# Attention values projected once per key block, and one MLP chunk computed by eight products instead of seven

## The reference, cut to what matters

```python
# attention, per layer; kv has 128 latent channels, 8 heads, w_uv[h] is 128 x 64
logits = einsum("bthc,btkc->bthk", q, kv_sel) * 128 ** -0.5 + bias
probs  = softmax(where(valid, logits, -inf))
o      = einsum("bthk,btkc->bthc", probs, kv_sel)   # 128 numbers per head
o      = einsum("bshc,hcd->bshd", o, w_uv)          # 64 numbers per head
x      = x + gate * rmsnorm(concat([y_conv, o * silu(g_attn)]) @ w_out)   # gate = part of silu(c) @ w_ada + b_ada
# MLP of the last layer, 1024 -> 4096 -> 1024
x      = x + square(relu(rmsnorm(x) @ w_up)) @ w_down
```

## Time and profile before

| | us |
|---|---|
| median of 3 runs (3002.47 to 3008.8) | 3005.6 |
| the profiled execution, device time | 3001.2 |
| its span in the trace | 2999.1 |
| PE busy with matmuls | 2766.2 (92%) |
| DVE busy | 2103.7 (70%) |
| ACT busy | 1417.0 (47%) |
| POOL busy | 1594.1 (53%) |

### The profile page before, as it was taken

One profiled execution on the slowest core, in us unless ns is written; L12 is line 12 of the kernel. 1 busy time (PEld: TensorE's weight loads), 2 busy tenths in 40 slices (PEclk: granted clock), 3 DMA queues, 4 the chain that ended last, 5 costly groups with the idle time before them and its releaser, 6 DMA issues.

```text
span 2999.1 us, 49452 instructions
## 1 busy us (share of the span) xinstructions
PE 2766.2 (92%) x19234; PEld 1706.8 (57%) x19442; DVE 2103.7 (70%) x3421; ACT 1417.0 (47%) x2541; POOL 1594.1 (53%) x1228
## 2 busy tenths in 40 slices
PE   6889989989879989989999999999999979999998
PEld 3459658754449668864566565665664434444443
DVE  5599987754599987644865665666654597777776
ACT  4366646533366746643344554454543343333333
POOL 4204669961504570012646956757662558888882
PEclk8999999999999999999999999999999989999999
DMA  7102433331202330022101211201123101111111
GB/s 274 46 1 86 141 102 120 101 131 50 95 1 81 123 118 23 23 82 78 43 29 43 71 43 32 82 29 57 57 74 124 57 29 57 57 57 56 57 57 63
DMA packets 50904, 213.49 MB, mean 71 GB/s; under 512 B 4680, under 2 KB 9968, under 8 KB 34032
## 3 DMA queue, kind: packets, MB, share of 16 engines
q1 hardware_dynamic: 42288, 195.63, 18.9%
q10 hardware_dynamic: 8384, 14.68, 1.5%
HBM read 190.36 MB, written 19.94 MB: 70 GB/s over the span
## 4 chain that ended last, share of the span: by engine, by line
PE 35%; DVE 8%; POOL 3%; issue 3%; ACT 1%; DMA 0%; DVEq 0%; ACTq 0%; POOLq 0%
PE big L303 8%; PE big L304 8%; PE big L302 7%; PE banks L1239 3%; PE banks L302 2%; PE banks L303 2%; PE banks L304 2%; POOL w_lo L638 2%; DVE arena L2899 2%; PE banks L1209 0%; PE banks L1218 0%; DVE arena L2880 0%; DVE arena L2805 0%; DVE arena L2726 0%; DVE arena L2884 0%
## 5 line engine op out<-in xcount | busy, mean ns | idle before, releaser
L725 POOL TENSOR_TENSOR w_lo<-stage,w_hi 128x512 bf16<-128x512 f32 x276 | 357.6, 1330 | 324.0 <-ACT w_hi L1475 323.7
L718 POOL CAST w_hi<-stage 128x512 bf16<-128x512 f32 x188 | 139.0, 782 | 592.2 <-PE big L304 465.0
L638 POOL TENSOR_TENSOR w_lo<-stage,w_hi 128x512 bf16<-128x512 f32 x174 | 249.6, 1445 | 260.9 <-ACT w_hi L1671 260.9
L302 PE MATMUL big<-w_hi,ht_hi 128*128 128x256 bf16 (+2 forms) x1272 | 352.5, 285 | 15.8 <-DVE ht_lo L2576 4.4
L303 PE MATMUL big<-w_lo,ht_hi 128*128 128x256 bf16 (+2 forms) x1274 | 353.5, 286 | 4.0 <-issue 3.7
L304 PE MATMUL big<-w_hi,ht_lo 128*128 128x256 bf16 (+2 forms) x1276 | 354.2, 286 | 0.3
L302 PE MATMUL big<-ht_hi,w_hi 128*128 128x512 bf16 x846 | 323.7, 383 | 26.2 <-POOL w_lo L638 8.5
L303 PE MATMUL big<-ht_lo,w_hi 128*128 128x512 bf16 x877 | 334.9, 382 | 12.5 <-DVE ht_lo L2154 10.1
L304 PE MATMUL big<-ht_hi,w_lo 128*128 128x512 bf16 x879 | 335.7, 382 | 1.0 <-issue 0.2
L303 PE MATMUL big<-arena,w_hi 128*128 128x512 bf16 (+1 forms) x783 | 249.2, 333 | 11.9 <-DVE arena L2323 8.0
L302 PE MATMUL big<-arena,w_hi 128*128 128x512 bf16 (+1 forms) x776 | 246.1, 332 | 14.9 <-DVE arena L2237 6.2
(11 more groups left out here) (416 smaller groups left out, 7795.0 us busy)
## 6 DMA issues: line engine op xcount, KB each, us to landing
stage<-in_w SPq DMA_DIRECT2D x130, 1024.0 KB, 4.9
arena<-in_w_ada SPq DMA_DIRECT2D x48, 512.0 KB, 3.9
arena<-in_x SPq DMA_DIRECT2D x16, 512.0 KB, 8.1
xs<-arena SPq DMA_DIRECT2D x16, 512.0 KB, 2.6
arena<-xs SPq DMA_DIRECT2D x16, 512.0 KB, 7.5
gt<-arena ACTq DMA_DIRECT2D x16, 256.0 KB, 2.8
arena<-gt ACTq DMA_DIRECT2D x16, 256.0 KB, 2.7
out_x<-arena SPq DMA_DIRECT2D x8, 512.0 KB, 2.6
```

The lines of the kernel that those rows point to most:

```text
L302: pe.matmul(out, ah, bh, start=start, stop=False, skip_group_check=onto)
L638: return pool.tensor_tensor(lo, x, hi, ALU.subtract)
L718: pool.tensor_copy(w_flat[0][:, w0 + c0:w0 + c1], stage[:, n % RAW_RING, c0:c1]).then_inc(s_w_hi_split, mark(s_w_hi_split, n, q))
L725: ins = pool.tensor_tensor(w_flat[1][:, w0 + c0:w0 + c1], stage[:, n % RAW_RING, c0:c1], w_flat[0][:, w0 + c0:w0 + c1], ALU.subtract)
```

## The change

1. Values. `values(s)` makes KV @ w_uv for key block s and all heads once (three matmuls of 512 columns), ahead of the loop for block 0 and after head 1 of block s-1 for the others; ACT and DVE split it into `VAL`. `weigh` now holds the probabilities still and streams 64 columns of `VAL`, all eight heads into one bank, one round later than before (i-4); `turn` is one round later too (i-2). The split of the weighed result, the 64-column product, its copy and the key transposes with their split are gone. `PB` gets a third buffer. DVE scales the whole block straight from PSUM. `turn_y` and the late sums move from the pool "big" to a bank of their own ("x").
2. Order. DVE does the low part of `PT` and of the queries ahead of the mask of the round; `turn_y` is at i-7.
3. Modulation. The group (0, 4) is computed at the start on PE by `ada_piece`, its four pieces loaded early; seven groups are left for POOL, which scales a piece by one tensor_tensor in place of two tensor_scalar, in rounds 20, 31, 39, 44, 51, 56, 63 in place of 20, 28, 36, 42, 48, 54, 58, 62. The gate row of layer 1 is multiplied at (1, 5), the last group.
4. MLP. Chunk 3 of `up` is computed by eight products; token sums 2 and 3 come after the first `down` pair.

```diff
-STRASSEN = range(3, 16)
+STRASSEN = range(4, 16)
-        pools = {..., "t": one[0:2], "o": one[2:4], "c": one[0:3], "f": one[3:4], "c2": two[2:4], "mlp": two}
+        pools = {..., "t": one[0:2], "o": one[2:4], "c": one[0:3], "pt": one[0:2], "ov": one[2:3], "x": one[3:4], "f": one[3:4], "c2": two[2:4], "mlp": two}
-        ADA_LATE = [(0, 4), (0, 5), (1, 4), (1, 5), (1, 0), (1, 1), (1, 2), (1, 3)]
-        ADA_STEP = dict(zip((20, 28, 36, 42, 48, 54, 58, 62), ADA_LATE))
+        ADA_LATE = [(0, 5), (1, 0), (1, 1), (1, 2), (1, 3), (1, 4), (1, 5)]
+        ADA_STEP = dict(zip((20, 31, 39, 44, 51, 56, 63), ADA_LATE))
...
 POOL, late_sums:
-                    for k in range(2):
-                        pool.tensor_scalar(x[:, k, :], x[:, k, :], s_(S_C + 2 * kp + k), None, ALU.mult)...
+                    pool.tensor_tensor(x, x, s_(S_C + 2 * kp, 2).unsqueeze(2).broadcast_to((P, 2, 512)), ALU.mult)...
 PE, transpose_x, behind the last transposes:
+                        if half and kp == 3:
+                            g = take(pe, "c", "gate4")
+                            for i in range(16, 20):
+                                ada_piece(i, g)
 PE, before the scores:
-                g = take(pe, "big", "kvtok", l)
-                for s in range(NT):
-                    ins = pe.transpose(g[:, s * P:(s + 1) * P], RAW[:, s * P:(s + 1) * P], ident)
 PE, attention:
+                def values(s):
+                    g = take(pe, "x", "v", l, s)
+                    mm3(pe, g, [x[:, s * P:(s + 1) * P] for x in KVT], [x[:, 0, 0:512] for x in uv], True, True)...
-                        ins = mm3(pe, g[:, 0:P], [x[:, s, :] for x in KVK], [x[:, s * P:(s + 1) * P] for x in PT[h % 2]], s == 0, s == tb)
+                        ins = mm3(pe, g, [x[:, s * P:(s + 1) * P] for x in PT[h % 2]], [x[:, s, h * 64:(h + 1) * 64] for x in VAL], s == 0, s == tb)
-                def values(tb, h, g):
-                    pe.wait_ge(s_ot_lo, when(s_ot_lo, l, tb, h))
-                    ins = mm3(pe, g[:, P:P + 64], OT[h % 2], [x[:, 0, h * 64:h * 64 + 64] for x in uv], True, True)
...
-                    if 3 <= i < n + 3:
-                        weigh(*steps[i - 3], g)
-                    if 5 <= i < n + 5:
-                        values(*steps[i - 5], g)
-                    if 1 <= i <= n:
-                        turn(*steps[i - 1])
+                    if 4 <= i < n + 4:
+                        weigh(*steps[i - 4])
+                    if 2 <= i < n + 2:
+                        turn(*steps[i - 2])
...
+                    if i < n and steps[i][1] == 1 and steps[i][0] < NT - 1:
+                        values(steps[i][0] + 1)
 ACT, MLP:
-                    evac(RT[n], ACT.Relu, "up", j, n, pool="mlp")
+                    evac(RT[n], ACT.Relu, "up", j, n, pool="mlp" if j < 3 else "big")
+                    sums_high("dn", 2, 0, 1, 2, 5, 4)
+                    token_sums(2, {2: lambda: sums_high("dn", 2, 3)})
+                    up_plain(3, (0,))
+                    token_sums(3, {1: lambda: sums_high("dn", 2, 6)})
+                    up_plain(3, (1,))
 DVE, MLP:
             token_sums(0)
             token_sums(1)
             square_parts(0)
-            token_sums(2)
             square_parts(1)
-            token_sums(3, lambda t: add_down(0, "p1", t - 3) if 3 <= t < 7 else None)
             for m in range(7):
                 down(m)
-                up_first(2 * m + 3)
+                if m:
+                    up_first(2 * m + 3)
+                else:
+                    square_low(2, "a22")
+                    token_sums(2)
+                    token_sums(3)
                 if m < 6:
                     up_second(2 * m + 4)
```

More of the change, by code:

```diff
@@ L603, in late_sums @@
             def late_sums():
-                for i in range(16, len(ADA_PIECES)):
+                for i in range(20, len(ADA_PIECES)):
                     l, n, kp = ADA_PIECES[i]
@@ L1089, in _ @@
                 queries(0)
-                for i in range(n + 8):
-                    if 8 <= i and steps[i - 8][1] == NH - 1:
-                        turn_y(steps[i - 8][0])
+                values(0)
+                for i in range(n + 7):
+                    if 7 <= i and steps[i - 7][1] == NH - 1:
+                        turn_y(steps[i - 7][0])
                     if i < n:
@@ L2489, in _ @@
                         late_part(*ADA_STEP[i - 1])
-                    if 2 <= i < n + 2 and steps[i - 2][0] >= 4:
-                        turned_lo(*steps[i - 2], 0)
+                    if 3 <= i < n + 3:
+                        tb, h = steps[i - 3]
+                        for q0 in range(0, tb + 1, 4):
+                            turned_lo(tb, h, q0)
+                        also(s_pt_lo, l, tb, h)
+                    if 1 <= i <= n and steps[i - 1][1] == 3 and steps[i - 1][0] < NT - 1:
+                        queries(steps[i - 1][0] + 1)
                     if i < n:
@@ L2505, in _ @@
-                    if 4 <= i < n + 4:
-                        tb, h = steps[i - 4]
-                        dve.wait_ge(s_ot_hi, when(s_ot_hi, l, tb, h))
-                        dve.tensor_tensor(OT[h % 2][1], tile("o", "o", l, i - 1)[:, 0:P], OT[h % 2][0], ALU.subtract).then_inc(s_ot_lo, mark(s_ot_lo, l, tb, h))
-                        freed(s_ot_lo, "o", l, i - 1)
-                    if i < n and steps[i][1] == 3 and steps[i][0] < NT - 1:
-                        queries(steps[i][0] + 1)
@@ new lines, in _ @@
+                    if 7 <= i and steps[i - 7][1] == NH - 1:
+                        tb = steps[i - 7][0]
+                        dve.wait_ge(s_ya_hi, when(s_ya_hi, l, tb))
+                        dve.tensor_tensor(ht_lo[:, 4:8, tb * P:(tb + 1) * P], tile("x", "yt", l, tb).rearrange("p (c t) -> p c t", c=4), ht_hi[:, 4:8, tb * P:(tb + 1) * P], ALU.subtract).then_inc(s_ya_lo, mark(s_ya_lo, l, tb))
+                        freed(s_ya_lo, "yt", l, tb)
+                    if 5 <= i < n + 5 and steps[i - 5][1] == NH - 1:
+                        tb = steps[i - 5][0]
+                        dve.wait_ge(s_yr, when(s_yr, l, tb))
```

202 lines of the change are left out of this document (103 added, 99 removed).

## The result

The changed kernel takes 2934.7 us as a median of four runs (2929.7 to 2941.0), where the kernel before takes 3006.5 in the runs beside it: a ratio of 0.9766 (95% interval 0.9747 to 0.9786), 71.8 us less. The profiled execution took 2930.5 with a span of 2928.7, 70.4 us less than the span before. The forecast was 2930, in a range from 2908 to 2960.

A forecast was written before the change was run, and what follows sets the result against it. PE's instruction list was taken to pace layer 1's attention loop, DVE the first MLP chunks. Terms -32 - 41 - 2.4 + 0 + 0 = -75 us on 3001.2 give 2926; with 4.4 for the median, 2930 (2908 to 2960).

The forecast's parts named there:

- only the columns: Rival, chance 0.22: both loops' idle time stays, POOL's new operation costs 3.2 us; median 2941 to 2960.
- the loads: Rival, chance 0.04: each 64-column matmul in `weigh` is paced by its own operand's load; up to 3049 at 98 ns.
- 864 x 26.6 = 23.0 us less of PE: Attention, each layer: all `weigh` matmuls drop from 55.6 to about 29 ns, taking 23.0 us off PE.
- where the prediction had put 5: Layer 1's loop: later rounds and a third `PB` buffer close 5 us (0 to 12) of PE's 16.3 idle.
- the change leaves this chain as it is: Loops, after head 3: the queries' chain PE, ACT, DVE stays a stall, masks 4.88 us apart, unchanged.
- POOL ends just ahead of PE and the loop takes 163 us: Layer 0's loop: POOL's 28 late pieces end at the lower end of 595 to 612; loop -39 us.
- the term for the late sums: Layer 0's loop: seven late sums and DVE's work on them add some 6 us to layer 1's 157.
- Costed at 0 with -2 as its better end: Start: the early group's eight float32 matmuls fit PE's idle wait at 61 to 70 us; 0 (-2 to +4).
- the term that halves the gain: Layer 0's tail: last gate sum and gate row multiply on DVE, some 3 us, eat half of 4, leaving -2.
- a forecast of 20 and 12.5: MLP, behind the first `down`: DVE takes 20 us for token sums 2 and 12.5 for sums 3.
- where over 10 had been named: MLP, inside `up` 4: PE waits over 10 us for DVE or ACT, as a sign of the forecast.

The follow-up runs named there:

- wide: Changed kernel, but `weigh` streams 128 columns of VAL instead of 64 for heads 0 to 6; 2956.2 us, 0.9841 of before.
- query_last: Changed kernel, but after head 3 PE makes the next query products at the end of its step, behind `weigh` and `turn`; 2920.4 us, 0.9718 of before.
- head3: Changed kernel, but at the seven steps with queries, ACT's exponential and queries' copy and DVE's queries' low part precede the transposes' work; 2920.3 us, 0.9715.
- pool_two: Changed kernel, but POOL scales each w_ada piece by two tensor_scalar of 512 columns instead of one tensor_tensor of 1024; 2931.7 us, 0.9762 of before.
- late_small: Changed kernel, but PE sums only 8 of the 512 columns of each late group; 2926.2 us, 0.9747 of before.
- gate_late: Changed kernel, but the first gate group is back among the late sums, eight of them, 32 pieces on POOL; 2937.7 us, 0.9776 of before.

## Why the prediction was right, and where it was not

**The time** came out within 5 us, and the loop of layer 1, both tails and the MLP within 4 each. The loop of layer 0 (-31.1 for -39.9) was in part made up for by the stretches ahead of it and by the one to the first `down`. That the total came so close is partly luck: in the loops the columns gave less than their term and the rest of the change more, and the start gave what had been put at nothing. The rival 'only the columns' had -27 for layer 1 with its tail and -31 for layer 0, where -28.4 and -31.1 came, and it was right that the idle time stays; its POOL price of 3.2 us was wrong, and it too counted the columns in full.

**Columns.** The price of the matmul was right: 29 ns apart in runs of up to 24 as in the bursts of three, so the rival 'the loads' fell. The Trainium skill (TensorE: Matmul & The Clock Gate, section Back-to-back issue gap) has about 81 ns for a sustained stream at 128 columns; the 56 ns of wide, where each matmul has a load of its own, speak against it here. What failed is the step "864 x 26.6 = 23.0 us less of PE": it takes every column as time of the loop. By wide a column added to this loop counts about 0.55 of itself. The other half of layer 1's gain, 13.3 us with head 7's columns, comes from the rest of the change, where the prediction had put 5; which part of it was not isolated.

**Stalls.** The step that failed is "the change leaves this chain as it is". Its links stayed, but `turn` moved behind the query products by one round and so brought the copy of the transposes and the exponential into the chain. The waits for the queries' low part became 12.9 and 10.5 us, the largest idle time left on PE in either loop, and taking most of it away is worth 8 us in layer 1 (query_last, head3) and 6 in layer 0 (head3). I had costed the shift of a round by what it releases, and not asked which in-order neighbour on ACT now waits for a later piece of PE's list.

**Layer 0 and POOL.** "POOL ends just ahead of PE and the loop takes 163 us" was wrong in its first half: the 1024-column tensor_tensor takes 1.89 us, under both ends of the range (2.6 and 3.2), the last piece is done at 580.7 instead of 595, and pool_two shows that even an end at 610 costs the loop no more than its spread. The loop took 171.9 all the same. Of the miss of 9 us, 3.3 are layer 1's too, and the rest is the term for the late sums, put at 6 where the two loops differ by 11.6. Its parts stay open: PE's products are some 2 of it by late_small, within the spread of that loop.

**Start.** Costed at 0 with -2 as its better end, it gave more: the first mask came 5.2 us earlier, of which 1.2 had been forecast for the key transposes, and gate_late takes 5.5 back, so some 4 within the spread of 3 between kernels. The mechanism was in the text, its size was not: the granted clock rose from 0.50 to 0.71 in the wait and from 0.88 to 1.00 in the 25 us behind it, some 3 us of PE's time (estimate from these two clocks). Where the rest arises stays open: the 192 matmuls of 8 columns start at 119.1 instead of 119.7, and in gate_late at 121.2.

**Tail of layer 0.** -2 was forecast and -0.1 came: the term that halves the gain was too small. DVE's wait for the last late sum, the gate sum and the multiply lie between mask and low parts, 3.1 us (607.0 to 610.1), and eat the whole gain and not half of it. In gate_late, where they are not in the tail, it takes 9.9 us, 4.8 less; that last late sum also comes a round earlier there, so the two are not parted. Layer 1's tail, without them, gave the -3.9.

**MLP.** Right in each step. Token sums 2 and 3 took 19.6 and 12.4 us for a forecast of 20 and 12.5. The first row of each and the operation behind the last:

```profile
2401.49 0.69 DVE L2834 TENSOR_TENSOR arena<-ht_hi 128x512 f32<-128x512 bf16 x1
2402.20 1.53 DVE L2835 TENSOR_TENSOR arena<-arena,ht_lo 128x512 f32<-128x512 f32 x1
...
2421.05 0.69 DVE L2834 TENSOR_TENSOR arena<-ht_hi 128x512 f32<-128x512 bf16 x1
2421.77 0.69 DVE L2835 TENSOR_TENSOR arena<-arena,ht_lo 128x512 f32<-128x512 f32 x1
...
2433.45 1.22 DVE L2862 SCALAR_TENSOR_TENSOR arena<-arena 128x1024 f32<-128x1024 f32 x1
```

The same operation (L2835) takes 1.53 us beside POOL's splitting and 0.69 without it. The Trainium skill (SBUF — State Buffer, section SBUF: two separate sides) gives the reason with the port pair that the prediction cites. The trace agrees: the two engines' operations start in turn there, POOL's at 2401.51 and 2403.26, DVE's at 2402.20 and 2403.77. The first `down` took 38.4 us instead of 53.2, and this gain came back behind it, with a wait of 11.5 us inside `up` 4, where over 10 had been named.

## What to carry to other kernels

When a step of a software pipeline is moved by a round, follow each in-order queue once more: what stands behind the moved piece there, and what that now waits for. A loop in which three engines hand work around may pay only a part of what is taken off the busiest one (here 11 us showed of 20 added), so test the exchange rate by adding work to it before counting columns. Two orders that each shorten one chain need not add; engines have to agree on which piece comes first.

## What was not expected

- POOL's tensor_tensor of 1024 float32 columns with a broadcast operand takes 1.89 us, less than 1.5 times one of 512 (1.28), and 40% less than two tensor_scalar of 512 (3.11).
- Work put into an idle wait of PE at the start shortened what follows it: the clock was granted in full from 70 us on instead of at 0.88, and the first mask came some 4 us earlier, for matmuls that cost nothing.
- The same swap on ACT (exponential ahead of copies) costs 32 us in layer 1 when made in all 64 steps and gains 8 when made in the seven that have the queries behind them.
